# Routing from the raw residual, and GpSimd for part of the normalisation

## The reference, cut to what matters

```python
x = x + gate1 * merged
h2 = rms_norm(x, norm_ffn) * (1 + scale2) + shift2
x = x + gate2 * grouped_moe(h2, w_router, router_bias, w_gate, w_up, w_down)
# in grouped_moe
scores = jax.nn.sigmoid((t @ w_router).astype(jnp.float32))
biased = scores + router_bias.astype(jnp.float32)
# the best of 4 groups of 4 experts by the sum of its two best, then its two best experts
w = w / jnp.sum(w, axis=-1, keepdims=True)
for e in range(N_EXPERTS):
    a = jax.nn.silu(t @ w_gate[e]) * (t @ w_up[e])
    out = out + gate[:, e:e + 1] * (a @ w_down[e])
```

## Time and profile before

| | us |
|---|---|
| median of 3 runs | 1531.93 |
| lowest, highest | 1531.48, 1536.96 |
| the profiled execution | 1532.77 |
| its span | 1530.9 |
| TensorE busy in the span | 1446.3 |
| VectorE busy | 1006.8 |
| ScalarE busy | 864.9 |
| GpSimd busy | 119.7 |

### The profile page before, as it was taken

The page is one execution under the profiler, slowest core; times in us unless marked ns, Lnnn a source line. Parts: engine busy times, 40 slices in busy tenths (PEclk is TensorE's granted clock), DMA queues, the critical chain, the costliest instruction groups (busy, mean ns, idle before and its releaser), DMA issues. The chain is left out here.

```text
span 1530.9 us, 19562 instructions
## 1 busy us (share of the span) xinstructions
PE 1446.3 (94%) x6948; PEld 1106.5 (72%) x6948; DVE 1006.8 (66%) x1258; ACT 864.9 (56%) x1242; POOL 119.7 (8%) x140
## 2 busy tenths in 40 slices
PE   7999989999989999999989999899998999999996
PEld 3777558887767777777567765687876777777774
DVE  1565685334388888888574848633355888888875
ACT  4632585323257777777564228732325677777764
POOL 0100000000021111211100000000000111111110
PEclk7999999999999999999999999999999999999998
DMA  9622761113359999999853148111235599999944
GB/s 359 217 96 96 274 221 56 56 55 110 107 189 357 363 371 361 357 354 358 325 221 110 55 180 315 56 56 55 95 126 216 211 372 366 367 368 358 362 177 169
DMA packets 148394, 341.25 MB, mean 223 GB/s; under 512 B 8308, under 2 KB 10634, under 8 KB 148201
## 3 DMA queue, kind: packets, MB, share of 16 engines
q1 hardware_dynamic: 136880, 317.20, 56.9%
q0 software_dynamic: 10720, 22.91, 4.0%
q10 hardware_dynamic: 728, 0.28, 0.1%
HBM read 332.82 MB, written 24.12 MB: 233 GB/s over the span
## 5 line engine op out<-in xcount | busy, mean ns | idle before, releaser
L799 PE MATMUL bank<-x_hi,w_lo 128*128 128x512 f32 x608 | 243.0, 400 | 9.6 <-DVE x_lo L2202 4.3
L800 PE MATMUL bank<-x_lo,w_hi 128*128 128x512 f32 x608 | 237.8, 391 | 0.0
L801 PE MATMUL bank<-x_hi,w_hi 128*128 128x512 f32 x608 | 237.7, 391 | 0.0
L2402 DVE TENSOR_TENSOR w_lo<-ring,x_lo 128x2048 fp32r<-128x2048 f32 x92 | 210.4, 2288 | 29.1 <-ACT x_lo L1680 28.6
L1680 ACT CAST zone_r<-ring 128x2048 fp32r<-128x2048 f32 x92 | 175.9, 1912 | 29.6 <-PE bank L1225 17.2
L1680 ACT CAST x_lo<-ring 128x2048 fp32r<-128x2048 f32 x92 | 176.0, 1918 | 26.6 <-PE bank L1240 14.6
L1223 PE MATMUL bank<-w_lo,zone_r 128*128 128x512 f32 x384 | 156.3, 407 | 0.3 <-issue 0.3
L1867 DVE TENSOR_TENSOR w_lo<-ring,w_hi 128x1024 fp32r<-128x1024 f32 x84 | 102.2, 1221 | 76.7 <-ACT w_hi L1400 75.9
L799 PEld LDWEIGHTS bank<-x_hi,w_lo 128*128 128x128 f32 x608 | 114.5, 188 | 41.0 <-issue 9.4
L800 PEld LDWEIGHTS bank<-x_lo,w_hi 128*128 128x128 f32 x608 | 114.6, 188 | 26.1 <-issue 2.4
L801 PEld LDWEIGHTS bank<-x_hi,w_hi 128*128 128x128 f32 x608 | 114.5, 188 | 24.5
(11 more groups left out here) (326 smaller groups left out, 2795.8 us busy)
## 6 DMA issues: line engine op xcount, KB each, us to landing
ring<-in_w_gate SPq DMA_DIRECT2D x32, 2048.0 KB, 13.6
ring<-in_w_up SPq DMA_DIRECT2D x32, 2048.0 KB
ring<-in_w_down SPq DMA_DIRECT2D x32, 2048.0 KB, 9.7
ring<-in_w_ada SPq DMA_DIRECT2D x24, 2048.0 KB, 12.2
ring<-in_w_in SPq DMA_DIRECT2D x16, 2048.0 KB, 8.6
ring<-in_w_out SPq DMA_DIRECT2D x4, 2048.0 KB, 7.8
zone<-y_by_choice SPq DMA_DIRECT2D x8, 1024.0 KB, 8.1
ring<-in_w_branch_a SPq DMA_DIRECT2D x2, 2048.0 KB, 9.1
```

The costliest lines, as they stand in the source:

```text
L799: mm(out, lo, x_first, start=start, stop=False)
L800: mm(out, hi, x_second, start=False, stop=False)
L801: return mm(out, hi, x_first, start=False, stop=stop)
L2402: v.tensor_tensor(w_low[EXPERT_SLOTS[par][k]][:, cols], ring[EXPERT_SLOTS[par][k]][:, cols], part_hi[buf].bitcast(F32), ALU.subtract)\
```

## The change

- Router: `w_router` is multiplied by the channel scales of each group (`route_w`) and by the shifts (`route_a`) on VectorE in the merge stage (`route_inputs`). One matmul with ones sums `route_a` over the channels ("route_add"), VectorE adds up its chunks (`route_sum`) to a constant per group. The routing products take raw `xT` as the stationary operand, 128 tokens at a time, and 16 columns of `route_w` as the moving one: 4 matmuls for a chunk, 32 in all. Chunks 0 and 1 come ahead of "mean2", 2 and 3 ahead of "spread2", 4 to 7 behind it. The three groups of warming matmuls (5, 4 and 3) are gone, also the logits' copy and their second product. VectorE multiplies the sums by the token's factor and adds the constant; ScalarE takes the sigmoid in place.
- Normalisation: ScalarE copies the spread tile from PSUM to SBUF (`wide_rstd`). VectorE multiplies chunks 0 to 4 only and waits for that copy first; ScalarE shifts them, three before the sigmoid and two after it. GpSimd multiplies and shifts chunks 5, 6 and 7.
- First gate weights: ScalarE rounds both halves after the row copies. VectorE's subtraction of half 0 moves from ahead of the choice to behind the selection tiles.

The diff, without declarations of tiles and semaphores:

```diff
@@ -339,12 +339,12 @@
             yield (gate if what == "gate" else y, j), (0, 1, 2, 3)
+    yield "route_add", (1,)
     for j in range(KC):
         yield ("out", j), (4, 5, 6, 7)
+    yield "router", (0,)
     yield "mean2", (3,)
     yield "spread2", (2,)
-    yield "router", (0,)
-    yield "scores", (1,)
     for half in range(2):
@@ -365,7 +365,8 @@
-SHIFT_ACT = (0, 2, 4, 5, 7)
+SHIFT_ACT = (0, 1, 2, 3, 4)
+SHIFT_POOL = (5, 6, 7)
 SCALE_DVE = (0, 4)
@@ -480,6 +481,9 @@
         rb = sb("rb", [P, NE])
+        route_const = part(0, GROUPS * NE).rearrange("p (g e) -> p g e", g=GROUPS)
+        route_w = rstd[:, 0:GROUPS * KC * NE].rearrange("p (g k e) -> p g k e", g=GROUPS, k=KC)
+        route_a = rstd[:, GROUPS * KC * NE:2 * GROUPS * KC * NE].rearrange("p (g k e) -> p g k e", g=GROUPS, k=KC)
         lam_s = part(10264, 6 * DEPTH).rearrange("p (i v l) -> p i v l", i=3, v=2)
@@ -1127,6 +1131,10 @@
                 nc.tensor.drain().then_inc(used[SLOT["brb"]], 1)
+                ps = take(layer_use, "route_add")
+                pe.wait_ge(S["route_ready"], 1)
+                done(layer_use, "route_add", mm(ps[:, 0:GROUPS * KC * NE], K("ones"),
+                                                route_a.rearrange("p g k e -> p (g k e)"), start=True, stop=True))
                 for j in range(KC):
@@ -1135,32 +1143,36 @@
                 before = pairs_until(pe, layer)
+                raw = take(layer_use, "router")
+
+                def route(k):
+
+                    b, n = layer_use[("out", k)]
+                    pe.wait_ge(free[b], n + 1)
+                    for t in range(TT):
+                        ins = mm(raw[:, t * NE:(t + 1) * NE], xT[:, k, t * P:(t + 1) * P], route_w[:, t // 2, k, :],
+                                 start=(k == 0 and t == 0), stop=(k == KC - 1 and t == TT - 1))
+                    return ins
+
+                route(0)
+                route(1)
                 ps = take(layer_use, "mean2")
-                keep_warm(ps, 5)
                 pe.wait_ge(S["sumsq_ready"], 1)
                 for t in range(TT):
                     ins = mm(ps[:, t:t + 1], tmp[:, 0, t * P:(t + 1) * P], K("ones")[:, 0:1], start=True, stop=True)
                 done(layer_use, "mean2", ins)
+                route(2)
+                route(3)
                 ps = take(layer_use, "spread2")
-                keep_warm(ps, 4)
                 pe.wait_ge(S["diag2_ready"], 1)
                 done(layer_use, "spread2", mm(ps[:, :], K("ones"), spread_diag.rearrange("p t n -> p (t n)"),
                                               start=True, stop=True))
-                ps = take(layer_use, "router")
-                keep_warm(ps, 3)
-                pe.wait_ge(in_pool, 16 * 2)
-                for k in range(KC):
-                    wait_h(pe, k)
-                    j = 32 * (k % 4)
-                    ins = mm(ps[j:j + NE, :], w_rout[:, k, :], hT[:, k, :], start=(k < 4), stop=(k >= KC - 4))
+                for k in range(4, KC):
+                    ins = route(k)
                 done(layer_use, "router", ins)
-                ps = take(layer_use, "scores")
-                pe.wait_ge(S["logits_ready"], 1)
-                for t in range(TT):
-                    ins = mm(ps[:, t * NE:(t + 1) * NE], logits[:, t * P:(t + 1) * P], K("by_expert"),
-                             start=True, stop=True)
-                done(layer_use, "scores", ins)
                 for half in range(2):
+                    for k in range(4 * half, 4 * half + 4):
+                        wait_h(pe, k)
                     for t in range(TT):
@@ -1647,16 +1659,12 @@
                         .then_inc(part_hi_ready, 1)
-                first_gate_high(0)
-                norm_shift()
-                ps = wait_full(act, use, "router")
-                nc.scalar.copy(logits, ps[:, :]).then_inc(S["logits_ready"], 1)
-                act.wait_ge(S["logits_ready"], 1)
-                nc.scalar.sem_inc(free[use["router"][0]], 1)
-                ps = wait_full(act, use, "scores")
-                af(sc[:, :, :].rearrange("p t e -> p (t e)"), ps[:, 0:TT * NE], ACT.Sigmoid).then_inc(S["score_ready"], 1)
-                act.wait_ge(S["score_ready"], 1)
-                nc.scalar.sem_inc(free[use["scores"][0]], 1)
+                ps = wait_full(act, use, "spread2")
+                nc.scalar.copy(wide_rstd, ps[:, :]).then_inc(S["spread_ready"], 1)
+                norm_shift(0, 3)
+                act.wait_ge(S["raw_ready"], 1)
+                af(sc[:, :, :], sc[:, :, :], ACT.Sigmoid).then_inc(S["score_ready"], 1)
+                norm_shift(3, len(SHIFT_ACT))
                 for half in range(2):
@@ -1664,7 +1672,8 @@
                         nc.scalar.sem_inc(free[use[("rows", t, half)][0]], 1)
-                first_gate_high(1)
+                for h in range(2):
+                    first_gate_high(h)
                 act.wait_ge(w_landed[0][1], earlier * 16 + 16)
@@ -1893,18 +1902,27 @@
             def norm_apply(own, wide_rstd):
-                for c in range(KC):
-                    ins = v.tensor_tensor(hT[:, c, :], xT[:, c, :], wide_rstd[:, :], ALU.mult)
-                    if c in SHIFT_ACT:
-                        ins.then_inc(S["xn_ready"], 1)
-                        continue
-                    own.step(ins)
-                    own.last()
-                    for g in range(GROUPS):
-                        h = hT[:, c, g * SEQ:(g + 1) * SEQ]
-                        ins = v.tensor_scalar(h, h, mul1[:, 1, c, g:g + 1], mod[:, 3 * KC + c, g:g + 1],
-                                              ALU.mult, ALU.add)
-                    ins.then_inc(S["h_ready_v"], 1)
+                for c in SHIFT_ACT:
+                    v.tensor_tensor(hT[:, c, :], xT[:, c, :], wide_rstd[:, :], ALU.mult).then_inc(S["xn_ready"], 1)
+
+            def route_inputs():
+
+                dve.wait_ge(in_pool, 16 * 2)
+                every = [P, KC, NE]
+                for g in range(GROUPS):
+                    v.tensor_tensor(route_w[:, g, :, :], w_rout[:, :, :],
+                                    mul1[:, 1, :, g].unsqueeze(2).to_broadcast(every), ALU.mult)
+                for g in range(GROUPS):
+                    ins = v.tensor_tensor(route_a[:, g, :, :], w_rout[:, :, :],
+                                          mod[:, 3 * KC:4 * KC, g].unsqueeze(2).to_broadcast(every), ALU.mult)
+                ins.then_inc(S["route_ready"], 1)
+
+            def route_sum(use):
+
+                ps = wait_full(dve, use, "route_add")
+                v.tensor_reduce(route_const[:, :, :], ps[:, 0:GROUPS * KC * NE]
+                                .rearrange("p (g k e) -> p g e k", g=GROUPS, k=KC), AX, ALU.add)\
+                    .then_inc(free[use["route_add"][0]], 1)
             def ada_sum(own, i):
@@ -2230,6 +2249,8 @@
                         low_part(OUT_GROUPS + W_BUFS + j)
+                    if j == 0:
+                        route_sum(use)
                     if j > 0:
@@ -2238,8 +2259,19 @@
                                 tok_rstd2.unsqueeze(2).to_broadcast([P, TT, P]), ALU.mult).then_inc(S["diag2_ready"], 1)
-                norm_apply(own, wait_full(dve, use, "spread2"))
-                own.last()
+                ps = wait_full(dve, use, "spread2")
+                dve.wait_ge(S["spread_ready"], 1)
+                norm_apply(own, ps)
+                ps = wait_full(dve, use, "router")
+                rowed = [P, TT, NE]
+                dve.wait_ge(free[use["route_add"][0]], use["route_add"][1] + 1)
+                own.step(v.tensor_tensor(sc[:, :, :], ps[:, 0:TT * NE].rearrange("p (t e) -> p t e", t=TT),
+                                         tok_rstd2.unsqueeze(2).to_broadcast(rowed), ALU.mult))
+                own.last()
+                v.sem_inc(free[use["router"][0]], 1)
+                by_group = sc[:, :, :].rearrange("p (g t) e -> p g t e", g=GROUPS)
+                v.tensor_tensor(by_group, by_group, route_const[:, :, :].unsqueeze(2).to_broadcast([P, GROUPS, 2, NE]),
+                                ALU.add).then_inc(S["raw_ready"], 1)
                 dve.wait_ge(S["xn_ready"], KC + len(SHIFT_ACT))
@@ -2252,8 +2284,6 @@
                                     ALU.subtract).then_inc(part_lo_ready, 1)
-
-                first_gate_low(0)
                 own.step(v.memset(picked[:, TT * NE:(TT + 1) * NE], 0.0))
@@ -2337,9 +2367,11 @@
                 v.sem_inc(free[use["ranks"][0]], 1)
+                dve.wait_ge(S["h_ready_p"], len(SHIFT_POOL))
                 for t in range(TT):
                     v.tensor_scalar(in_first[:, t, :], K("place"), rank[:, t * NE:t * NE + 1],
                                     picked[:, t * NE:t * NE + 1], ALU.is_equal, ALU.mult).then_inc(S["first_ready"], 1)
+                first_gate_low(0)
                 count = rank[:, TT * NE:(TT + 1) * NE]
@@ -2564,6 +2596,15 @@
                         pool.dma_start(bias[:, :, t, :], src).then_inc(rel_back, 16)
```

(9 more changed lines are left out.)

11 lines of the change are left out of this document (6 added, 5 removed).

## The result

| | before | after |
|---|---|---|
| median of 7 runs, us | 1531.48 | 1543.88 |
| lowest, highest | 1527.81, 1536.96 | 1540.94, 1549.38 |
| the profiled execution | 1532.77 | 1543.95 |
| its span | 1530.9 | 1542.1 |
| GpSimd busy in the span | 119.7 | 129.1 |

The ratio of after to before is 1.0083, 95% interval [1.0066, 1.0099]: slower by 0.8%, more than the half per cent that can be told from no change. The median was forecast at 1539.1 and came 4.8 us above it: inside the range of 1529 to 1547, but above the 1535 to 1542 that the forecast gave its own mechanism. The most likely outcome on record was no change that can be told (0.60); slower had 0.35.

What follows compares the result with a forecast made beforehand. TensorE's pace bounds the long phases; changes elsewhere count only where it waits or changes clock. Full-clock -2.6, map +4.2 and routing +5.6 gave +7.2 us: 1539.1 on the median 1531.93 (1540.0 on the profiled 1532.77), range 1529 to 1547.

Steps and rivals of the forecast that it cites:

- its own mechanism: Main forecast: half clock in both the routing stretch and the map; 1535 to 1542 us, chance 0.48.
- The cast on the path: Before the map: the moved subtraction delays the place tile, so TensorE waits 4.1 us; at full clock the sum is -2.6.
- Rival 3: Choice to experts: early scores survive, L1195 starts 4.6 us earlier and all behind follows; 1522.5 us, chance 0.05.
- Half clock in both places: Routing products and map: TensorE's granted clock falls to 0.50 in both layers.
- map term: Map and L1195 matmuls at half clock: +2.1 us per layer against full clock, +4.2 in all.
- Rival 1: Routing stretch: clock holds or falls only at its end, 1533.5 to 1536; full clock everywhere, 1529.3; chance 0.31 (0.12 everywhere).
- routing term: Routing products to row copies: half clock from near B+4 (B: last output matmul's end), +2.8 us per layer, +5.6.
- its sign: Start of the choice of experts (L2261): about 3 to 6 us nearer to the last output matmul's end.
- rival 2: Row transposes: slow GpSimd, above 2.9 us per chunk, makes their second half wait; 1544 us at 4.0, chance 0.16.
- The merge stage: Added VectorE products and the 0.48 us matmul are hidden in waits: taken as 0, without cover 2 to 3 per layer.
- GpSimd: hidden, as forecast: Normalisation: GpSimd's three chunks, 2.0 us each, stay hidden behind ScalarE; they cost from 2.9 us per chunk.
- mutual blocking: Choice of experts: GpSimd and VectorE exclude each other for whole instructions; choice loses at most 2 us, sum unchanged.

Runs made afterwards that it cites:

- early_cast: The changed kernel with only the first gate weights' cast and subtraction (half 0) put back ahead of the choice: 1535.31 us, ratio 1.0012 to the kernel before.
- before_late_cast: The kernel before with only half 0's cast moved behind the row copies and its subtraction behind the selection tiles: 1545.23 us, ratio 1.0079.
- shift_first: early_cast with ScalarE shifting all five of its chunks before the sigmoid: 1532.38 us, ratio 1.0008 to the kernel before.
- norm_on_vector: The changed kernel with chunks 5, 6 and 7 normalised by VectorE instead of GpSimd: 1547.12 us, ratio 1.0107 to the kernel before.
- logits_first: shift_first with router weights stationary, logits copied directly behind the spread copy, VectorE's subtraction in the wait for ranks: 1528.36 us, ratio 0.9978 to the kernel before.

## Why the prediction was right, and where its sizes were off

**The cast on the path: right, and it decides.** The step was that VectorE's subtraction would stand between the selection tiles and the chain to the place tile. The wait ahead of the map was forecast at 4.1 us and is 3.45 and 3.36. early_cast shows that without it the change is worth 1.0012, and before_late_cast that it costs 1.0079 alone. Rival 3 (the early scores survive) falls with the selection tiles at B+25.8 and B+25.6: not even those came earlier.

**Half clock in both places, in both layers: right.** The map term was forecast with the rest of the way from the place tile to the gathered rows at 12.35 us (45.9 - 33.55); it measures 12.4 in both layers. (The prediction takes +2.1 for the map, where its own 2.9 less 0.5 are 2.4; layer 0 shows 2.2.) In the routing the clock falls at B+4.9 and B+4.8, as forecast near B+4, but stays down to B+22, not B+18. Rival 1, in both its forms, falls with it.

**The routing term: mis-sized.** The forecast was +2.8 us per layer, last row copied at B+23.1. Measured is B+24.3 and B+24.0, and by this the place tile is 1.25 and 0.95 us late and all behind it. The spread came earlier than forecast (8.1 and 7.8 for 9.7), the choice 1.1 and 0.5 later; it is 2.0 and 2.7 us nearer to B than before, less than the 3 to 6 that the prediction named as its sign. The selection tiles were to come at 20.9 + 2.8 = B+23.7 and are 2.1 and 1.9 late; that does not show behind them, because VectorE waits for the cast then. What the prediction left out is the wait of the transposes for the fourth chunk: ScalarE shifts it behind the sigmoid, so TensorE stood for 2.16 us and then turned rows at 0.85 us per bank, at half clock, slower than ScalarE can copy. shift_first takes that wait away, and the rows come 2.1 us earlier, at B+22.1.

**The sum.** The forecast was +7.2 us, the spans differ by 11.2. The stretch accounts for 2.3 of the missing 4.0 (9.5 against 7.2). The other 1.7 lie outside it, where the prediction had nothing: 0.8 and 2.4 us at "route_add", 2.5 less ahead of it that are no effect of the change, and 1.0 elsewhere that no run explains. The remaining 0.8 of the 4.8 us between the forecast and the median is what the profiled execution of before lay above its median. The forecast lay only half a microsecond below the border of half a per cent, so either error alone was enough to carry the result across it. The range reached up to 1547 for the sake of rival 2, a slow GpSimd, which did not come; that the median lies inside it is in part luck.

**The merge stage: put at nothing, and it costs.** The prediction called the new matmul hidden, because it stands before an output group in which TensorE waits 1.66 us for VectorE, and took 0 for it; a merge stage that gets longer was one of its signs of being wrong. The sign came. The matmul's own time was not what mattered: it waits 2.80 us for its bank, in both layers of all eleven kernels that have it, and the output matmuls behind it, which need nothing from that bank, wait with it. From the start of the last emptying of bank 1 to B the three kernels without it take 44.7 to 44.8 us in all six stretches; the eleven with it take 45.5 where the clock stays full (8 stretches) and 47.0 to 47.2 where it falls for 3.4 us there (14 stretches, layer 1 of after among them; none of the six without it has such a fall). So it costs 0.8 or 2.4 us per layer. No run gave the product another bank or another place, so that this is the cause is read from the traces and not tested.

**GpSimd: hidden, as forecast.** A chunk is 1.28 + 1.10 = 2.4 us, against 2.0 taken and 2.9 from which it would cost. The Trainium skill (GPSIMD Engine Reference, Performance versus the Vector engine) gave a ratio of 1.96, from which I had an estimate of 2.7; the 512 wide product measures 1.28 against VectorE's 0.64, a ratio of 2.0, the pair of scalings 1.10 against 0.73, a ratio of 1.5. By that rule the product agrees, and the scalings do not. Rival 2 falls; norm_on_vector shows the part's sign, a gain of 0.9 to 1.0 us per layer.

**The mutual blocking: no cost in after, some in its variants.** The prediction allowed 2 us of it for the choice. VectorE's five products beside GpSimd's work take 3.08 us, 0.62 each, their time alone; one of their inputs is a PSUM bank. The choice's first operation is 0.23: it starts at 428.92, when GpSimd has just ended its last scalings (427.73 + 1.14 = 428.87). Where the order made the choice start beside a GpSimd product it took 1.34.

**Where the gain of the change went.** The choice starts 2.0 and 2.7 us earlier, and nothing behind it does: the transposes wait for a shift, the row copies for the transposes at half clock, and the subtraction does the rest. Put right step by step (cast early, one or more shifts moved ahead of the sigmoid, two chunks on GpSimd, weights stationary), the same idea ends at 0.9971 [0.9957, 0.9984], 4.4 us less than before by that ratio. That is below half a per cent, though the interval lies below 1. Its stretch is 2.6 and 3.5 us shorter than before, and 2.4 us per layer of that go again at "route_add". I moved the subtraction twice, once into the path again (logits_first), and never the matmul that waits for its bank, so what this form can reach is open.
